# Phase ends without waits for their stores, and gate products in blocks of six in an RWKV-7 and attention layer

## What is computed

```python
h = rms_norm(x); att, rcols, g_r = split_projection(h @ w_in)
# attention heads: 8 heads of 64, chunks of 64 that see 8 chunks back, relative bias, softmax
# RWKV heads, after token shift and two small (64-wide) decay and key-rate products:
def step(S, inp):
    r_t, w_t, k_t, v_t, kk_t, a_t = inp
    sa = jnp.einsum('bhij,bhj->bhi', S, -kk_t)
    S = (S * w_t[:, :, None, :] + sa[..., None] * (kk_t * a_t)[:, :, None, :]
         + v_t[..., None] * k_t[:, :, None, :])
    return S, jnp.einsum('bhij,bhj->bhi', S, r_t)
y = group_norm(ys) * gn_g + gn_b + sum(r * k * r_k) * v
o_r = y * silu(g)
out = x + concatenate([o_a * silu(g_A), o_r]) @ w_out
```

## Time and profile before

| | |
|---|---|
| median of 3 runs | 1806.29 us (1805.58 to 1806.95) |
| profiled execution | 1801.65 us, of which span 1799.9 |
| mean granted clock of PE | 0.976 of full |
| PE busy | 1707.6 us, 95% |
| DVE, ACT, POOL busy | 822.9, 801.2, 412.9 us |
| HBM traffic | 113.21 MB read, 55.06 MB written |

### The profile page before, as it was taken

One profiled execution on the slowest core, in us unless ns is written; L12 is line 12 of the kernel. 1 busy time (PEld: TensorE's weight loads), 2 busy tenths in 40 slices (PEclk: granted clock), 3 DMA queues, 4 the chain that ended last, 5 costly groups with the idle time before them and its releaser, 6 DMA issues. The chain is left out here.

```text
span 1799.9 us, 48546 instructions
## 1 busy us (share of the span) xinstructions
PE 1707.6 (95%) x21338; PEld 1399.9 (78%) x21338; DVE 822.9 (46%) x1196; ACT 801.2 (45%) x1657; POOL 412.9 (23%) x283
## 2 busy tenths in 40 slices
PE   6899999999997999999789999999999998969999
PEld 5688888888886888999667777777777776647787
DVE  4244445444444411222346565555655556624332
ACT  5465666666654422223434444444444443324320
POOL 3322212222110000000213444334443342310000
PEclk9899999999998999999889999999999998979999
DMA  5312111112134322214211212212121123356652
GB/s 213 109 68 76 52 60 70 44 63 89 44 108 165 137 80 85 84 63 145 88 64 51 70 51 74 57 51 70 51 74 57 51 80 130 109 208 233 212 167 92
DMA packets 119137, 170.87 MB, mean 95 GB/s; under 512 B 39568, under 2 KB 78992, under 8 KB 118672
## 3 DMA queue, kind: packets, MB, share of 16 engines
q1 hardware_dynamic: 109568, 153.29, 25.9%
q10 hardware_dynamic: 9360, 14.49, 2.2%
HBM read 113.21 MB, written 55.06 MB: 93 GB/s over the span
## 5 line engine op out<-in xcount | busy, mean ns | idle before, releaser
L620 PE MATMUL a_ps_proj<-a_w_hi,a_x_hi 128*128 128x512 f32 x384 | 156.8, 408 | 7.4 <-ACT a_qk L403 7.4
L620 PE MATMUL a_ps_proj<-a_w_hi,a_x_lo 128*128 128x512 f32 x384 | 150.9, 393 | 0.0
L620 PE MATMUL a_ps_proj<-a_w_lo,a_x_hi 128*128 128x512 f32 x384 | 150.4, 392 | 0.0
L1020 DVE SCALAR_TENSOR_TENSOR j_out<-j_ps,j_rest,j_part 128x512 f32<-128x512 f32 (+2 forms) x65 | 41.9, 644 | 219.0 <-ACT j_last_cols L966 172.5
L543 DVE SCALAR_TENSOR_TENSOR a_stage<-a_ps_s,a_new_bias 128x256 f32<-128x256 f32 x64 | 27.2, 425 | 242.5 <-PE a_ps_s L647 242.5
L2133 PE MATMUL r_ps_gate<-gate_w_hi,gate_x_hi 128*128 128x512 f32 x272 | 116.7, 429 | 7.8 <-POOL r_kiclr_rest L1479 6.0
L2133 PE MATMUL r_ps_gate<-gate_w_lo,gate_x_hi 128*128 128x512 f32 x272 | 116.2, 427 | 0.0
L2133 PE MATMUL r_ps_gate<-gate_w_hi,gate_x_lo 128*128 128x512 f32 x272 | 115.8, 426 | 0.0
L964 ACT ACTIVATE j_part<-j_last_cols,j_shift_in 128x1 f32<-128x1 f32 x65 | 19.2, 295 | 211.7 <-PE j_ps L1045 211.7
L1791 DVE TENSOR_TENSOR r_w_mat<-r_ps_w,consts 128x512 f32<-128x512 f32 x83 | 57.3, 691 | 106.9 <-PE r_ps_w L2017 106.9
L2447 PE MATMUL o_ps_y<-out_w_hi,o_z_hi 128*128 128x512 f32 x240 | 98.0, 408 | 2.5 <-DVE o_z_lo L2370 2.5
(11 more groups left out here) (340 smaller groups left out, 4481.0 us busy)
## 6 DMA issues: line engine op xcount, KB each, us to landing
a_xT<-in_x_T SPq DMA_DIRECT2D x17, 512.0 KB, 3.4
scratch_xT<-a_xT SPq DMA_DIRECT2D x17, 512.0 KB, 2.7
raw<-scratch_xT SPq DMA_DIRECT2D x17, 512.0 KB, 4.1
scratch_gates<-r_gate_out SPq DMA_DIRECT2D x34, 256.0 KB, 2.4
z_gate<-scratch_gates SPq DMA_DIRECT2D x17, 512.0 KB, 3.9
xs<-scratch_xs_T SPq DMA_DIRECT2D x15, 576.0 KB, 4.5
a_x<-in_x_prompt SPq DMA_DIRECT2D x16, 512.0 KB, 6.3
scratch_xs_T<-j_out ACTq DMA_DIRECT2D x39, 192.0 KB, 1.9
```

Source lines behind the costliest of these rows:

```text
L620: mm = nc.tensor.matmul(ps_proj[:], a[n % 2][:, k, :], w[:, k, g * AW:(g + 1) * AW], start=(k == 0 and i == 0), stop=(k == KT - 1 and i == 2))
L1020: last = nc.vector.scalar_tensor_tensor(out=out[j][:, 0:n], in0=ps[j][:, 0:n], scalar=rest[:, c:c + 1], in1=part[j][:, 0:n], op0=ALU.mult, ...
```

## The change

Two things are done together.

*Phase ends.* The semaphores of the stores of keys, values, attention output, mixed columns, shift rows, states and gates move to `Shared`; waits for stores leave the ends of the phases and stand where the memory is first overwritten or read: in the projection phase ahead of ACT's and DVE's second weight split and SP's load 7, in the recurrence ahead of SP's first gate weights, ACT's first copy and the first gate copy, in the output phase before the last tile's load and at the end. In attention xT has a third buffer, its load goes three tiles ahead, and `split_hi(2)` and `norm_stats(2)` stand later in tile 0. PE's wait for parameters moves from the start of the recurrence to its first use.

*The recurrence.* Gate products go in blocks of 6 (the last of 12). kk_sum and the turns of v move from mix(t + 2) to front(t + 1). x_hi and x_lo of the gates have two buffers, the gates' x is loaded two tiles ahead, its splits on ACT and POOL move from keys 32.6 and 33.7 to 24.8 and 26. xs comes in one load a tile instead of two. Keys change throughout, the order of jobs in the banks with them. The diff, cut to its core:

```diff
 # Shared
+        self.k_stored, self.v_stored, self.new_stored, self.att_stored = (sem(n + "_stored") for n in ("k", "v", "new", "att"))
+        self.xs_stored, self.shift_stored = [sem(f"xs_stored{i}") for i in range(2)], sem("shift_stored")
+        self.o_stored, self.wkv_stored, self.y_stored = sem("o_stored"), sem("wkv_stored"), [sem(f"y_stored{i}") for i in range(2)]
 # attention_phase, SP
             def load_xT(n):
-                wait(sp, xT_stored, 16 * (n - 1))
-                sp.dma_start(xT[n % 2][:], io["x_T"][n]).then_inc(xT_loaded[n % 2], 16)
+                wait(sp, xT_stored, 16 * (n - 2))
+                sp.dma_start(xT[n % 3][:], io["x_T"][n]).then_inc(xT_loaded[n % 3], 16)
...
             load_x(1)
+            load_xT(2)
...
-            sp.wait_ge(k_stored, 16 * 4)
-            sp.wait_ge(v_stored, 16 * 4)
-            sp.wait_ge(new_stored, 16 * 4)
-            sp.wait_ge(xT_stored, 16 * (TILES + 1))
-            sp.wait_ge(out_stored, 16 * TILES)
 # attention_phase, ACT
                 exps(t, 1)
-                if t == 0:
-                    split_hi(2)
-                    norm_stats(2)
...
                 read_pT(t, 2)
+                if t == 0:
+                    split_hi(2)
+                    norm_stats(2)
                 exps(t, 3)
 # rwkv_projection_phase
-            sp.wait_ge(last_stored, 16)
...
+            kept(act)
             split_w(1)
...
-            for c, j, i in blocks(GROUPS):
-                act.wait_ge(stored[j], 16 * (i + 1))
...
             split_w(1)
+            kept(dve)
 # rwkv_phase
-        JOB_ORDER = ((("bonus", -1), ("decay", 0), ("k_tok", -1), ("B0", -1), ("B1", -1), ("v_tok", 0)),
-                     (("iclr", 0), ("b_tok", -1), ("K0", -1), ("K1", -1), ("kk_sum", 0), ("v_swap", 0)))
+        JOB_ORDER = ((("v_tok", -1), ("bonus", -1), ("decay", 0), ("k_tok", -1), ("B0", -1), ("B1", -1)),
+                     (("kk_sum", -1), ("v_swap", -1), ("iclr", 0), ("b_tok", -1), ("K0", -1), ("K1", -1)))
...
-        LEVEL_AT, CHAIN_AT = 4.1, (20.5, 26.85)
-        GRAM_AT = (25.05, 28.15)
+        LEVEL_AT["p"], CHAIN_AT["p"], SOLVE_AT["p"], READ_AT["p"], U_AT["p"] = 4.8, (22.5, 27.9), (23.6, 30.5), (26.1, 33.5), (24.3, 31.2)
+        LEVEL_AT["s"], CHAIN_AT["s"], SOLVE_AT["s"], READ_AT["s"], U_AT["s"] = 4.1, (20.5, 26.85), (22.9, 29.25), (26.2, 32.4), (23.7, 30)
+        GRAM_AT, GATE_AT = (24.4, 26.8), ((3.3, 6), (8.1, 6), (12.9, 6), (17.7, 6), (28.9, 6), (31.3, 6), (34.2, 12))
 # rwkv_phase, SP
                 for j in range(2):
-                    yield (13.2, 33.5)[j]
+                    yield (20.3, 37.4)[j]
                     store_gates(t, j)
-                    if j == 0 and t < DEC:
-                        sp.wait_ge(x_lo_ready, t)
-                        load_gate_x(t + 1)
+                    if j == 0 and t + 2 <= DEC:
+                        sp.wait_ge(x_lo_ready, t + 1)
+                        load_gate_x(t + 2)
...
+            def front(t, u, mode):
+                yield 15
+                if t + 2 <= DEC:
+                    need(sp, t, "rkr", "rhat")
+                    for name in ("iclr", "v_tok", "v_swap"):
+                        was_written(sp, t + 1, name)
+                    load_xs(t + 2, u)
...
-            sp.wait_ge(stored, 16 * (1 + NCH))
-            sp.wait_ge(o_stored, 64 * (TILES + 1))
+            sp.wait_ge(o_stored, 64 * TILES)
 # rwkv_phase, POOL
             def gates(t, u, mode):
                 if t < DEC:
-                    yield 33.7
+                    yield 26
                     split_x(t + 1)
 # rwkv_phase, ACT
             def gates(t, u, mode):
-                for j in range(2):
-                    yield (12.4, 32.5)[j]
-                    copy_gates(t, j)
+                yield 19.4
+                copy_gates(t, 0)
                 if t < DEC:
-                    yield 32.6
+                    yield 24.8
                     split_x(t + 1)
+                yield 37.2
+                copy_gates(t, 1)
 # rwkv_phase, DVE
                 for name, out, n in (("B0", bm, 0), ("K0", km, 0), ("B1", bm, 1), ("K1", km, 1)):
-                    yield GRAM_AT[n] + 1.2
+                    yield {"B0": 26.2, "K0": 26.3, "B1": 28, "K1": 28.1}[name]
...
                     for n in range(NCH):
-                        yield (25.3, 31.7)[n]
+                        yield (26.05, 33.4)[n]
                         dve.wait_ge(s_written, 2 * t + n + 1)
...
                     for n in range(NCH):
-                        yield (28, 37.5)[n]
+                        yield (28, 43)[n]
                         dve.wait_ge(dec_written, n + 1)
 # rwkv_phase, PE
-                yield 31.4
+            def front(t, u, mode):
+                yield 1.1
                 need(pe, t, "kk_sq")
                 ps, done = free_bank(t, "kk_sum")
                 nc.tensor.matmul(ps[:], const("head_ones"), kk_sq[:], start=True, stop=True).then_inc(done, 1)
-                yield 35.3
+                yield 5.9
                 turn_two(t, "v_tok", xs[u][:, 8:12], "v_swap", xs[u][:, 8:12])
-            def front(t, u, mode):
-                yield 11.5
+                yield 10.7
                 need(pe, t, "rkr")
...
-                    yield (24.5, 30.9)[n]
+                    yield (25.5, 32.9)[n] if mode == "p" else (24.5, 30.9)[n]
                     pe.wait_ge(u_ready, 2 * t + n + 1)
...
             def gates(t, u, mode):
-                for j, keys in enumerate(((1.1, 3.2, 5.2, 7.3, 9.3, 11.4), (13.4, 17.5, 19.6, 23.6, 28.9, 30))):
-                    for b, key in enumerate(keys):
-                        yield key
-                        gate_products(t, j, b)
+                done = 0
+                for key, count in GATE_AT:
+                    yield key
+                    gate_products(t, done, count)
+                    done += count
 # output_phase, SP
                 if n == LAST:
+                    sp.wait_ge(shared.o_stored, 64 * (TILES + 1))
```

More of the change, by code:

```diff
@@ L147, in attention_phase @@
         x_tok = at("x", [P, D], AT_XT)
-        xT = [at(f"xT{i}", [P, KT, P], AT_RAW + i * D) for i in range(2)]
+        xT = [at(f"xT{i}", [P, KT, P], word) for i, word in enumerate((AT_RAW, AT_RAW + D, AT_XT + D))]
         x_hi, x_lo = ([sb(f"x_{n}0", [P, KT, P], F32R), at(f"x_{n}1", [P, KT, P], AT_XT + (2 + i) * D, F32R)]
@@ L183, in attention_phase @@
         w_hi_ready, w_lo_ready = sem("w_hi_ready"), sem("w_lo_ready")
-        x_loaded, xT_loaded = sem("x_loaded"), [sem(f"xT_loaded{i}") for i in range(2)]
+        x_loaded, xT_loaded = sem("x_loaded"), [sem(f"xT_loaded{i}") for i in range(3)]
         x_sumsq, x_logms, x_rstd = sem("x_sumsq"), sem("x_logms"), sem("x_rstd")
@@ L809, in weights @@
             return parts
-        w_hi, w_lo = weights("hi", 0), weights("lo", 1)
+        w_hi = weights("hi", 0)
+        out = [sb(f"out{i}", [P, GT * P]) for i in range(2)]
+        w_lo = weights("lo", 1)
         w_raw, xT = shared.raw, shared.shift_x
@@ L817, in rwkv_projection_phase @@
         part = [sb(f"part{i}", [P, 1 + GT * P]) for i in range(2)]
-        out = [sb(f"out{i}", [P, GT * P]) for i in range(2)]
         shift_in, rest = sb("shift_in", [P, SHIFT_TILES, 1 + NS]), sb("rest", [P, SHIFT_TILES])
@@ L1282, in gate_block @@
             return ap.rearrange("p k n -> p (k n)").rearrange("p (k n) -> p k n", k=2)
+        XS_STORES = [(5 * SHIFT_TILES + 1 - j) // 2 for j in range(2)]
         def nothing(t, u, mode):
@@ L1348, in _ @@
             last_w = len(gate_blocks) - 1
+            for j in range(2):
+                sp.wait_ge(shared.xs_stored[j], 16 * XS_STORES[j])
             sp.wait_ge(x_lo_ready, 1)
@@ L1428, in out @@
                     load_x_half(1, j)
-            def mix(t, u, mode):
-                if t < 2:
-                    return
-                yield 0.1
-                was_written(sp, t - 1, "v_tok")
-                past(sp, t - 1, "rkr")
-                load_xs(t, u, slice(4, CT), xs_loaded)
-                yield 20
-                past(sp, t - 1, "rhat")
-                load_xs(t, u, slice(0, 4), r_loaded)
+                yield 50
+                for j in range(2):
+                    store_y(1, j)
+            def front(t, u, mode):
[5 more added lines that the diff above has]
+                    load_xs(t + 2, u)
             def tail(t, u, mode):
@@ L1460, in back @@
                                      states[:, :, now, :].rearrange("p c b d -> p c (b d)")).then_inc(stored, 16)
-            tiles(sp, nothing, back, mix, tail, gates, first_gates, out)
-            for j in range(2):
-                store_y(1, j)
-            for j in range(2):
-                sp.wait_ge(y_stored[j], 16 * 2)
-            sp.wait_ge(stored, 16 * (1 + NCH))
-            sp.wait_ge(o_stored, 64 * (TILES + 1))
+            tiles(sp, front, back, tail=tail, gates=gates, first_gates=first_gates, out=out)
             for j in range(2):
```

(21 more changed lines are left out.)

159 lines of the change are left out of this document (84 added, 75 removed).

## The result

The changed kernel takes 1873.59 us (median of 4 runs, 1870.61 to 1878.8), the kernel before 1806.62 beside it: a ratio of 1.0365 (95% interval 1.0342 to 1.0389), 67 us slower. The profiled execution has a span of 1872.3 against 1799.9.

What follows compares the result with a forecast made beforehand. PE was taken to bound the recurrence loop, busy 590.6 of 599 us. Sixteen tiles at 41.25 instead of 37.3 us (+63.2), less 21.7 outside the loop, gave +41.5 and 1848 us; range 1786 to 1859.

Steps and rivals of the forecast that it cites:

- Part 3: Recurrence loop: POOL's earlier split starts 0.45 us before DVE's multiplication and holds it, +1.85 us a tile.
- Part 2: Recurrence loop: PE waits 2.05 us a tile before the second key-product group for DVE's reads; an old 0.26 wait goes.
- The v_tok wait: Recurrence loop: the bonus group waits for v_tok's bank, +0.46 us a tile.
- The rival with POOL too late: Recurrence loop: POOL starts too late to hold DVE's multiplication, PE waits 2.05 us a tile; kernel 1792 us, chance 0.24.
- the clock's term: Recurrence loop: PE's 4 us idle in each tile lowers its clock for 3.3 us, +1.65 us a tile.
- Part 5, attention: Attention start: the third buffer lets the load go early and removes PE's 7.40 us idle, -8.5 us.
- Part 5, the sample tile: Tile 16 of the recurrence: its loads are issued behind a later gate copy, +0.8 us.
- The sum of the loop: Recurrence loop: a tile period of 41.25 us instead of 37.3, over sixteen tiles +63.2 us.
- Part 1: Recurrence loop: gate products in seven blocks instead of twelve save 0.36 us a block, -1.80 us a tile.
- The seams: Between phases, without store waits: attention to projection -2.2 us, projection to recurrence -3.0, recurrence to output -7.0.
- The prologue: Before the recurrence's first state update: head sums and turns leave it, -1.8 us.

Runs made afterwards that it cites:

- pool_late: The changed kernel with POOL's split of the gates' x put back from key 26 to 33.6: 1827.13 us, ratio 1.0100 to the kernel before.
- reads_first: The changed kernel with DVE reading the first key products ahead of the state's addition and multiplication: 1815.36 us, ratio 1.0039 to the kernel before.
- eight_held: The changed kernel with eight gate blocks instead of seven, POOL's and DVE's orders as in the change: 1834.12 us, ratio 1.0157 to the kernel before.
- Experiments 9 to 11: The kernel before with the new phase ends, and attention as changed (1802.44 us), with split and statistics at their old place (1801.55), or its old loop (1802.76).
- act_key: The changed kernel with ACT's copy after a q group put back to 3.2 from 3.35 for the sample tile alone: 1861.96 us, ratio 1.0292 to before.
- experiment 5: Also called seven_moved: as eight, but the gate block at key 22.4 put back to the end, making seven blocks: 1799.38 us, ratio 0.9962 to the kernel before.
- both: The changed kernel with POOL's split at key 33.6 and DVE's reads ahead of the state's update: 1805.98 us, ratio 0.9987 to the kernel before.
- eight: The kernel of both with eight gate blocks of six, two of them inside the stretch of small products: 1791.97 us, ratio 0.9903 to the kernel before.
- twelve: The kernel of eight with its four blocks of six in the levels cut into eight of three, twelve blocks: 1794.33 us, ratio 0.9941 to the kernel before.

## Why the prediction was right and wrong

**Right in mechanism.** Part 3, the hold, is the change's main cost, and pool_late and reads_first show it. In a tile where POOL starts 0.38 ahead of the multiplication (forecast 0.45) PE's wait grows from 1.80 to 3.62, by 1.82 for the forecast 1.85. Part 2's wait was 1.80 for 2.05, of which 0.17 is a difference of measure: the walk counts from where the next product could start, the profile's idle time from the end of a product (0.63 for a group whose successor follows after 0.46). The v_tok wait is 0.44 for 0.46. As POOL is earlier in six tiles, the hold is less on the mean: of the 2.9 us a tile between the changed kernel and pool_late 1.5 are the wait (3.21 against 1.74) and 1.8 are the clock, by which the same products keep PE busy 37.62 instead of 35.84, less 0.4 of gaps (0.55 against 0.91). Forecast were 1.85 and 1.65. The rival with POOL too late is what pool_late measures: 1827, not 1792. It named the point that decides most of the time, but not the sign, because the sample tile, attention and the gaps were missing from it too.

**The size of the clock's term is in part luck.** The 3.3 us were read from one stretch of 5 us, as the shortest time at the lower level. In the trace of before they are the end of a longer one, which began at 53.1, while PE still stood (stretches as in the earlier trace rows):

```profile
53.00:55.00 2.00, 0.00 (x0) 0.00 (x0) 0.00 (x0) 0.00 (x0) 1.02 (x1) 0.52 0.81 266
55.00:60.00 5.00, 1.19 (x3) 0.99 (x4) 0.55 (x1) 4.37 (x9) 2.34 (x1) 0.50 0.55 210
60.00:63.00 3.00, 3.00 (x9) 2.32 (x8) 0.83 (x2) 1.45 (x7) 0.00 (x0) 0.50 0.01 0
63.00:65.00 2.00, 1.94 (x12) 1.17 (x10) 0.01 (x1) 0.00 (x0) 0.00 (x0) 0.92 0.00 0
```

In the changed kernel a fall lasts 3.4 us and costs, by eight_held, 1.3 to 1.4, less than the 1.65; but four of them last twice as long and one tile has two, so that the mean is 1.8. The two errors nearly cancel.

The Trainium skill ("SBUF — State Buffer", summary of rules) gave the hold with the multiplication ending its own 0.42 behind POOL's end, the row of L1760 gave 0.55; measured are 0.29 in the changed kernel and 0.28 in eight_held. That row's operation has twice the elements in each partition, and half of its 0.55 is what was measured. That a read from PSUM isn't held could not be seen in the earlier trace rows, as POOL stood idle then; the addition in eight_held shows it (last section).

**Wrong, by three steps, 9 to 12 us each.**

1. Part 5, attention, -8.5, measured +3.1: "The third buffer lets the load go early". It did, and the time did not come. The forecast counted the split's new place as 1.0 and did not ask what SP does next: x of tile 3 waits in SP's queue behind a row that is stored and loaded back (9.4 us from 60.92), and that behind the landing of a stored xT, in the same order as in the kernel before. Neither the third buffer nor the place of `norm_stats(2)` changes the order of these steps. Idle time moved, from 7.40 to 12.35. Experiments 9 to 11 bear it out: three versions, one time.

2. Part 5, the sample tile, +0.8, which measured +11 beyond the extra period. The forecast walked the prompt tile key by key and took the sample tile's order from the diff's own list of unchanged keys. The 0.15 on one key of ACT let the copy fall behind seven steps of another generator. act_key gives 12 to 13 us back for it.

3. The sum of the loop, 41.25 for 42.0. The gaps (0.55 a tile against 0.16 before) were in no term: the forecast took the supply of PE's instructions as free. The trace of before has four gaps, and experiment 5 shows what they are. Another 0.2 of the mean is the last period, 44.5, in which tile 16's loads begin.

**Right sign, size somewhat high.** Part 1's -1.80 for five blocks fewer is -1.4 by PE's busy time in periods without gaps: 36.9 before, 35.5 with seven blocks (the period from 1417.02 on in seven_moved and its like in pool_late and both, the only ones without even a small stall at the places of the gaps), 35.9 in eight, 36.6 in twelve. So the eighth block costs the forecast 0.36 and a block cut in two half of that. In the times of the kernels it doesn't show, since fewer blocks bring more gaps; eight blocks are faster than seven. Part 2's remark that nothing takes up the wait held: it goes only by a block at the right place, 26.5, or by DVE reading first.

The seams came as forecast: -2.2, -3.75 and -6.1 for -2.2, -3.0 and -7.0. The prologue gave twice its -1.8.

## What to carry to other kernels

When an order written by hand is changed, look at each two-input SBUF operation of VectorE on the critical path and at what GpSimd runs in the same microsecond: a background job of 2.4 us that started 0.4 us ahead of such an operation cost some 46 us here, and nothing at its old place. Give a shared buffer back before updating what nobody waits for yet, and spread large products so that they stand in long runs of small ones: there PE can run through its instructions faster than they are fetched, and the blocks' place was worth more (15 us) than their number (7 us for four blocks). An idle time without a releaser can be looked up by counting the engine's instructions and comparing it with the landings of the instruction queue. A wait that is removed shows its gain only if the next resource in the chain comes sooner too; and a key changed for one mode must be checked against every generator it is merged with in the other.

## What the runs showed of the hardware

- VectorE's multiplication of two SBUF operands, 0.42 us alone, took 2.25 to 2.29 when it started 0.37 to 0.38 behind a GpSimd subtraction of 2.34 to 2.38, and ended 0.28 to 0.29 behind it. The addition just ahead of it, with one operand in PSUM, took 0.42 with the same GpSimd operation running (eight_held: 1057.62, GpSimd from 1057.70).
- TensorE's granted clock fell in one of fifteen tiles with an idle time of 1.80 in nearly every tile (pool_late), in eight of fifteen with one of 2.08 (eight_held), and in all fifteen with 2.04 to 3.63 (the changed kernel). Two idle times of 0.55 and 0.70 a few us apart left it at 0.99. A fall lasted 3.4 us, in some tiles 6.8, and one of 3.4 cost 1.3 to 1.4 us.
- TensorE's instructions came in packets of 16 KB, one for 256 products and weight loads. It stood 0.2 to 2.7 us in 133 places of fourteen loops, always at the same place in a count by 256 and until 0.96 to 1.62 us after a packet had landed. That was 0.55 to 0.91 us a tile where small float32 products ran for 8 us or more without a large one between them, 0.12 to 0.16 a tile where a block of six large products cut the stretch, and 0.16 to 0.49 in the old order.
